# Adding the mask of the decay matrices on VectorE instead of multiplying it in on TensorE

## The reference

```python
a_cs = jnp.cumsum(dtc * a, axis=2)
seg = a_cs[:, :, :, None] - a_cs[:, :, None, :]
lower = jnp.tril(jnp.ones((L, L), dtype=bool))[None, None, :, :, None, None]
decay = jnp.exp(jnp.where(lower, seg, -jnp.inf))
cb = jnp.einsum('bclgn,bcsgn->bclsg', cc, bc)
y_diag = jnp.einsum('bclsg,bclsgr,bcsgrp->bclgrp', cb, decay, xd)
...
y = y_fwd + y_bwd + xs * d_skip
```

## Time and profile before

| | before |
|---|---|
| median of 3 runs | 1845.61 us (1844.77 to 1845.63) |
| the profiled execution's own time | 1845.08 us |
| span of the profiled execution | 1843.3 us |
| TensorE busy | 1828.3 us (99%) |
| TensorE weight loads busy | 1628.1 us (88%) |
| VectorE busy | 1266.7 us (69%) |
| ScalarE busy | 1055.9 us (57%) |
| granted TensorE clock | 1.00 over the whole span |

### The profile page before, as it was taken

How to read it: one execution, slowest core, us unless ns; L and a number is a source line. 1 busy time by engine, 2 the same in 40 slices (tenths; PEclk the granted TensorE clock), 3 DMA queues, 4 the chain that set the end, 5 groups by cost and what they waited for, 6 DMA issues and landing times.

```text
span 1843.3 us, 28625 instructions
## 1 busy us (share of the span) xinstructions
PE 1828.3 (99%) x11626; PEld 1628.1 (88%) x11626; DVE 1266.7 (69%) x1944; ACT 1055.9 (57%) x1557; POOL 100.5 (5%) x85
## 2 busy tenths in 40 slices
PE   9999999999999999999999999999999999999999
PEld 9998998789998999899789998988878888887887
DVE  6764797766665665588876665687667567875755
ACT  6444767565444444576755544475776456568642
POOL 0000110000000000020000000002001000210100
PEclk9999999999999999999999999999999999999999
DMA  8555542345555556553325555554445555534553
GB/s 292 193 191 182 188 151 100 106 137 189 192 193 186 190 195 194 180 179 112 126 92 172 191 193 189 173 184 147 139 137 182 194 163 182 171 126 137 172 192 116
DMA packets 86596, 310.09 MB, mean 168 GB/s; under 512 B 9648, under 2 KB 10288, under 8 KB 86464
## 3 DMA queue, kind: packets, MB, share of 16 engines
q1 hardware_dynamic: 85680, 306.35, 50.7%
q0 software_dynamic: 496, 1.65, 0.2%
q10 hardware_dynamic: 288, 0.25, 0.0%
HBM read 307.16 MB, written 1.05 MB: 167 GB/s over the span
## 4 chain that ended last, share of the span: by engine, by line
PE 95%; ACT 3%; DVE 1%; issue 0%; DMA 0%; POOL 0%; SPq 0%; DVEq 0%; ACTq 0%
PE bank L1162 92%; PE bank L1159 3%; ACT PA L1579 1%; DVE PA L2686 0%; ACT MP L1579 0%; ACT WH L1579 0%; ACT L1579 0%; DVE WL L2034 0%; DMA X<-in_x_dram 0%; ACT ET L1579 0%; DVE PC L2711 0%; DVE STATS L2384 0%; ACT BZ L1579 0%; DVE BO L2676 0%; DVE X L2120 0%
## 5 line engine op out<-in xcount | busy, mean ns | idle before, releaser
L2034 DVE TENSOR_TENSOR WL<-RAW,WH 128x1024 fp32r<-128x1024 f32 x585 | 704.6, 1213 | 405.0 <-ACT WH L1579 403.4
L1579 ACT ACTIVATE WH<-RAW 128x1024 fp32r<-128x1024 f32 (+2 forms) x587 | 610.1, 1050 | 497.0 <-PE bank L1162 494.2
L1162 PE MATMUL bank<-WH,FR 128*128 128x512 f32 x1264 | 318.4, 390 | 0.0
L1162 PEld LDWEIGHTS bank<-WH,FR 128*128 128x128 f32 x1264 | 233.7, 188 | 48.4 <-issue 0.8
L1162 PE MATMUL bank<-XTH,WH 128*128 128x256 f32 x1792 | 254.4, 279 | 0.6 <-ACT XTH L1579 0.6
L1162 PE MATMUL bank<-XTH,WL 128*128 128x256 f32 x1792 | 251.9, 278 | 0.0
L1162 PE MATMUL bank<-XTL,WH 128*128 128x256 f32 x1792 | 251.1, 277 | 0.0
L1162 PEld LDWEIGHTS bank<-XTH,WH 128*128 128x128 f32 x1792 | 226.9, 188 | 1.5 <-issue 0.8
L1162 PEld LDWEIGHTS bank<-XTH,WL 128*128 128x128 f32 x1792 | 226.7, 188 | 0.0
L1162 PEld LDWEIGHTS bank<-XTL,WH 128*128 128x128 f32 x1792 | 226.0, 188 | 0.0
L1162 PE MATMUL bank<-WL,FR 128*128 128x512 f32 x632 | 173.7, 389 | 0.0
(11 more groups left out here) (337 smaller groups left out, 1850.6 us busy)
## 6 DMA issues: line engine op xcount, KB each, us to landing
RAW<-in_WALL_dram SPq DMA_DIRECT2D x569, 512.0 KB, 3.3
RAW<-in_WALL_dram SPq DMA_DIRECT2D x8, 448.0 KB, 3.3
RAW<-in_WALL_dram SPq DMA_DIRECT2D x8, 256.0 KB, 2.6
X<-in_x_dram SPq DMA_DIRECT2D x4, 256.0 KB, 5.5
out_dram<-X SPq DMA_DIRECT2D x4, 256.0 KB, 2.0
ROWP<-in_ROWP_dram POOLq DMA_DIRECT2D x1, 672.0 KB, 11.0
CONSTS<-in_CST_dram POOLq DMA_DIRECT2D x1, 664.0 KB, 7.9
ROUNDED<-in_CSTR_dram POOLq DMA_DIRECT2D x1, 208.0 KB, 12.2
```

Source lines behind the costliest of these rows:

```text
L1162: return self.e.matmul(out, lhs, rhs, start=start, stop=stop, skip_group_check=True)
L1579: return self.e.activation(out, in_, func, **k)
L2034: self.e.tensor_tensor(lo, raw, hi.bitcast(F32), ALU.subtract).then_inc(*self.up("lo", j))
```

## The change

The mask product on TensorE goes. The bank is laid out by head, then direction, so that the two `TO` products write contiguous halves and the first of them opens the accumulation; the other two now write strided. VectorE reads the finished bank, adds the mask (broadcast over the two heads) and writes ET in SBUF: this is the VectorE part of `seg`, and it, in place of ScalarE's exponential, frees the bank and waits for the slot of ET. ScalarE exponentiates ET in place. That and the two operations of VectorE that follow make a new phase `exps`, which the planner places by itself. The costs that the planner sees change with it, from P53 A61 V90 in one phase to P40 V71 and A61 V90.

```diff
-"seg": "P53 A61 V90"
+"seg": "P40 V71", "exps": "A61 V90"
-    "seg": "exp"
+    "exps": "exp"
-FREES = {"seg": "A", "as": "V"}
+FREES = {"as": "V"}
...
         def segment(n):
             yield [("seg", i, n)]
+            yield [("exps", i, n)]
             if n:
                 yield "apply", i, n - 1
...
     # TensorE
-        b, bank = self.tbank(("seg", i, n), "et_act", (i, n))
-        ps = bank[:, :].rearrange("p (d x s) -> p d x s", d=2, x=2)
+        b, bank = self.tbank(("seg", i, n), "cut_dve", (i, n))
+        ps = bank[:, :].rearrange("p (x d s) -> p x d s", d=2, x=2)
-        self.mm(ps, k.EYER, k.CUT.unsqueeze(2).to_broadcast([128, 2, 2, 128]), True, False)
...
-            self.mm(ps[:, :, x, :], k.TO[:, h0 + x:h0 + x + 1].to_broadcast([128, 128]),
-                    k.LBH[:, 256 * t:256 * t + 256].rearrange("p (d s) -> p d s", d=2), False, False)
+            self.mm(ps[:, x, :, :], k.TO[:, h0 + x:h0 + x + 1].to_broadcast([128, 128]),
+                    k.LBH[:, 256 * t:256 * t + 256].rearrange("p (d s) -> p d s", d=2), x == 0, False)
...
     # apply reads the sum of the directions at columns 256 * x instead of 128 * x
...
     # ScalarE
-    def seg(self, i, n):
-        w.wait_ge(*self.at("seg_pe", (i, n)))
-        if n >= 4:
-            w.wait_ge(*self.at("apply_pe", (i, n - 4)))
-        else:
-            w.wait_ge(*self.at("fin_pe", (i, 1, 1)))
-        self.act(k.ET[:, n % 4, :], k.PS[k.bank["seg", i, n]][:, :], ACT.Exp).then_inc(*self.up("et_act", (i, n)))
+    def exps(self, i, n):
+        w.wait_ge(*self.at("cut_dve", (i, n)))
+        self.act(k.ET[:, n % 4, :], k.ET[:, n % 4, :], ACT.Exp).then_inc(*self.up("et_act", (i, n)))
...
     # VectorE
+    def seg(self, i, n):
+        cut = k.CUT.rearrange("p d s -> p (d s)").bitcast(F32).unsqueeze(1).to_broadcast([128, 2, 256])
+        w.wait_ge(*self.at("const5", 0))
+        w.wait_ge(*self.at("seg_pe", (i, n)))
+        if n >= 4:
+            w.wait_ge(*self.at("apply_pe", (i, n - 4)))
+        else:
+            w.wait_ge(*self.at("fin_pe", (i, 1, 1)))
+        e.tensor_tensor(k.ET[:, n % 4, :].rearrange("p (x e) -> p x e", x=2),
+                        k.PS[k.bank["seg", i, n]][:, :].rearrange("p (x e) -> p x e", x=2), cut, ALU.add).then_inc(
+            *self.up("cut_dve", (i, n)))
```

More of the change, by code:

```diff
@@ L190 @@
 TABLE = {
-    "decay0": "exp", "decay3": "log", "ex": "exp", "sc": "exp", "seg": "exp", "cn_a": "sqrt", "conv_silu": "silu",
+    "decay0": "exp", "decay3": "log", "ex": "exp", "sc": "exp", "exps": "exp", "cn_a": "sqrt", "conv_silu": "silu",
     "silu": "silu", "evict_z": "silu", "rope": "sin", "chain0": "exp", "chain7": "exp", "lam0": "exp", "mse": "exp",
@@ L1442, in apply @@
             h = 8 * g + 2 * q + x
-            m = self.mm(k.PS[t][:, 64 * (h % 8):64 * (h % 8) + 64], k.ET[:, n % 4, 128 * x:128 * x + 128],
+            m = self.mm(k.PS[t][:, 64 * (h % 8):64 * (h % 8) + 64], k.ET[:, n % 4, 256 * x:256 * x + 128],
                         k.XS[:, t, 64 * h:64 * h + 64], h % 8 == 0, True)
@@ L1568, in program @@
             "cn_split": self.cn_split, "qk_sq": self.qk_sq, "qkt": self.qkt, "sc": self.sc, "pt": self.pt, "mo_sq": self.mo_sq, "cum": self.cum,
-            "ex": self.ex, "xs": self.xs, "btk": self.btk, "cbm": self.cbm, "state": self.state, "seg": self.seg,
+            "ex": self.ex, "xs": self.xs, "btk": self.btk, "cbm": self.cbm, "state": self.state, "exps": self.exps,
             "fin_y": self.fin_y, "fin_norm": self.fin_norm, "chain": self.chain, "lam": self.lam, "hconv": self.hconv,
@@ L1996, in program @@
             "mo_a": self.mo_a, "mo_var": self.mo_var, "mo_y": self.mo_y, "cum": self.cum,
-            "state_x": self.state_x, "fin": self.fin, "seg": self.seg, "skip": self.skip, "mid": self.mid, "fin_y": self.fin_y,
+            "state_x": self.state_x, "fin": self.fin, "seg": self.seg, "exps": self.exps, "skip": self.skip, "mid": self.mid, "fin_y": self.fin_y,
             "fin_var": self.fin_var, "ift": self.ift, "chain": self.chain, "lam": self.lam, "rope2": self.rope2,
@@ L2444, in fin, with exps @@
             *self.up("fin_dve", (i, t, g, 0)))
+    def exps(self, i, n):
+        k, w, e = self.k, self.w, self.e
+        g, t = n // 8, n // 4 % 2
+        two = k.ET[:, n % 4, :].rearrange("p (x e) -> p x e", x=2)
+        own = two[:, :, 0:128]
+        w.wait_ge(*self.at("et_act", (i, n)))
+        e.tensor_tensor(own, own, two[:, :, 128:256], ALU.add).then_inc(*self.up("et_dve"))
+        w.wait_ge(*self.now("et_dve"))
+        w.wait_ge(*self.at("cbm_act", i))
+        e.tensor_tensor(own, own, k.CB[:, t, g, :].unsqueeze(1).to_broadcast([128, 2, 128]), ALU.mult).then_inc(
+            *self.up("et_dve", (i, n)))
     def seg(self, i, n):
         k, w, e = self.k, self.w, self.e
[L2448 to L2456, removed]
+        cut = k.CUT.rearrange("p d s -> p (d s)").bitcast(F32).unsqueeze(1).to_broadcast([128, 2, 256])
[8 more added lines that the diff above has]
+            *self.up("cut_dve", (i, n)))
     def skip(self, i, t):
```

2 lines of the change are left out of this document (1 added, 1 removed), and 2 rows, old and new, of the table WORK.

## The result

The changed kernel takes 1859.67 us (median of 4 runs, 1859.30 to 1861.64) against 1845.44 us for the kernel before (4 runs): the ratio is 1.008, interval 1.0068 to 1.0093, so 14.2 us slower. The forecast was 1842.1 us, its range ended at 1847.5, and 0.10 stood on slower.

The account below looks back on a forecast made before the run. TensorE, busy 99%, was taken as the bound: 7.0 us of masks saved, half lost waiting for VectorE, so 3.5 us off the median 1845.6 gives 1842.1 us. The 8-in-10 range was 1838.0 to 1847.5.

Parts of the forecast that it names:

- VectorE's balance: Each mixer's segment window: 40.0 us of VectorE work at 95.5 to 98.9% busy, a gain of 1.0 to 2.5 us.
- The length of the way: Segment's way from TensorE to its apply: 1.45 us before, 2.14 after, covered by a 2.5 us block; nothing taken.
- outer bound, 15 us: Segments' longer way, if uncovered: 0.47 us for each of 32, 15 us in all; chance 0.03.
- Splits leaving: Each mixer's segment window: three of VectorE's seven splits leave, taking out 3.7 us, made up behind it.
- third rival: Mixers: VectorE becomes the bound and costs more than the masks, splits staying in the window; 1846.6 to 1851.4 us, chance 0.16.
- The masks: TensorE in both mixers: 32 mask products removed at 0.22 us each, 7.0 us saved in all.
- The clock: Both mixers' segment windows: granted clock 1.00, playing no part in the sum.
- Outside the window: Behind each segment window: splits made up where VectorE has 5.3 us free; no added TensorE idle time counted.
- The durations: Segments: VectorE additions of 0.69 us, ScalarE exponential 0 to 0.04 us longer than 595 ns, sum of directions unchanged.
- fourth table load: ScalarE in each mixer: a possible further table load of 1.28 us beyond three, put at 0; a sign of being wrong.

Follow-up runs that it names:

- j1: Kernel before without its mask product, old order, plus an unawaited VectorE product of 512 constant columns behind each segment's product with cb; 1858.92 us, ratio 1.0068.
- e1: Kernel before without its mask product, nothing in its place, every engine in the old order; 1842.12 us, ratio 0.9978.
- h4: Kernel before without its mask product, old order, plus a VectorE product with ones and zeros between exponential and sum; 1863.36 us, ratio 1.0097.
- j2: Kernel before without its mask product, old order, plus a GpSimd fill of 640 columns between exponential and sum; 1849.71 us, ratio 1.0022.
- h3: Changed kernel with the splits of either mixer's segments moved back by two in the order; 1859.41 us, ratio 1.0075.
- e2: Changed kernel, same order, with the mask product put back on TensorE as well, so the mask is added twice; 1860.79 us, ratio 1.008.
- f1: Changed kernel, TensorE and VectorE order kept, exponential straight from the bank, an equal VectorE addition left that nobody waits for; 1868.28 us, ratio 1.0126.
- f2: Changed kernel, TensorE and VectorE order kept, exponential straight from the bank, addition dropped, no mask anywhere; 1863.63 us, ratio 1.0098.

## Why the prediction was wrong

**The step that failed: VectorE's balance.** "VectorE is busy 32.69 us of it and has 10.2 us free" took for free what has a price. 7.4 of those 10.2 us stand in the earlier trace rows as idle time ahead of the sums, ended by ScalarE's exponentials. The prediction showed this row and used its durations alone. Such time can be filled only by making the sums, and with them the apply, late: the changed kernel filled it (0.1 us left), and TensorE idled 4.4 us in each stretch and 3.2 and 2.8 behind it, where 1 to 2.5 us a mixer were forecast. In j1, against e1, VectorE did 7.8 us more in the first stretch (40.7 for 32.9), and the stretch grew by 5.9 us. The prediction then asked how full VectorE can get and took 95.5 to 98.9% from the stretch ahead of the segments. In the stretch itself it reached 89% in the changed kernel, with 47.2 us of work in place of 40.0, 85% in j1 and 83% in h4. With 40.0 us of work, 89 to 85% make a stretch of 44.9 to 47.1 us, 2 to 4 us a mixer longer than before in place of 1.0 to 2.5 shorter. These shares hold the lowered clock too: without the estimated 1.6, 5.3 and 5.0 us that it cost, they would be 91, 96 and 92%. How full VectorE could get at a clock of 1.00 throughout is therefore open.

**The length of the way.** "The length alone is covered" and "I take nothing for the length" were the second failure: j2 puts it at 5.8 us for 1.2 us more of way, 0.63 us of it the fill itself. The way was also mis-sized: 1.45 us before and 2.14 after add up the durations alone, while the runs have 1.9 and 4.4, with the waits in the queues. The prediction's outer bound, 15 us, was never part of a rival but for a chance of 0.03.

**Splits leaving.** Three were to leave the stretch; ten were made in it in place of seven, while three blocks of products moved in. The sign that the prediction named for the third rival, seven splits and a window over 42.9 us, came, and was exceeded. But h3, with one split fewer in each stretch, gained nothing.

**The masks.** 7.0 us were forecast, 3.5 came out (e1), and in the changed kernel 1.1 to 3.5 (e2). The Trainium skill's figure, by which the prediction had put the masks at an estimated 4.2 us ("TensorE: Matmul & The Clock Gate", "Back-to-back issue gap"), lies within the interval of 2.4 to 5.9, and mine doesn't. That doesn't bear the figure out, since the rows show 0.21 us and more a product and none shows 131 ns. What the runs do show is that the clock was lowered in both stretches of e1; the second, TensorE alone, beside the first above:

```profile
921.67:963.54 41.87, 40.88 (x238) 0.96 0.27 88
```

0.04 x (41.90 + 41.87) = 3.4 us went back there (an estimate), and idle time rose from 15.0 to 1840.7 - 1824.4 = 16.3 us. With the clock's share added back the masks come to 6.9 us. So the price of a product was about right, and what the sum lacked was the clock.

**The clock.** "The granted clock is 1.00 in both and plays no part" held for the kernel before alone. By the mean granted clock of the span, 0.996, the changed kernel loses some 0.004 x 1858 = 7 us to it (an estimate, since the clock is given to three digits). That is as much as the masks were to give, and its busy time didn't fall with them. So three terms make up the 14 us: the masks' 7 us less, the clock's 7 us more, and 14.2 us more of idle time.

**Outside the window.** The 3.2 and 2.8 us of idle time behind the stretches weren't in the sum: three blocks that stood there before had moved into the stretches.

**What was right.** The durations (684 ns forecast as 690, the exponential 632 as up to 631, the sum unchanged), no fourth table load in the stretch, nothing outside the mixers, and that VectorE's queue decides. The third rival had that mechanism, with the price of over-full work alone, 1846.6 to 1851.4 us; without the way, the crossings and the clock it ended 8 us short.

**What stays open.** The shares in the changed kernel's own order. Why the clock falls in one run and not in another is open, too. In the old order load and way are 14.9 and 5.8 us of the 20.5; in the new one f1 and f2, which were meant to part them, were spoiled by an order made for other work. How far a still better order could go wasn't settled by eight; that none beat 1857.9 us, and that a step of 0.63 us on the idle GpSimd alone already took 1849.7 us (j2), speaks against this change in any form tried here. No version that does the whole work beat the kernel before.

## What to carry to other kernels

Before work is moved to an engine with free time, look in its groups at what ends that idle time: waits in an in-order queue for a partner that works in turns with it are no free room, since work put there makes the partner's chain late. A step put into a chain with few items under way costs twice, by its load on the engine and by its length, and here the two added up to within some 3 us; measure them apart by putting the load behind the chain, and the length on an engine that has nothing to do. Read the granted clock beside every such comparison: waiting and a lowered clock are two costs. And when an order is written out beforehand, an experiment that removes work must let it be written anew or start from the order that was fitted to what is left.

## What the hardware did that I had not expected

**How much idle time a stretch holds doesn't tell what the clock does.** f2_no_add idled 7.0 us in the first stretch at a clock of 1.00 throughout and 7.0 us in the second at 0.97; e1_no_mask idled 1.0 us at 0.96. In e1 TensorE was busy 1.73 us of 364 to 366 and throughout from 366 to 368, and in the latter the clock fell; in the first stretch of f2 it was busy 3.06 and 3.23 of 5, and the clock stayed. First e1, then f2, with its second stretch last:

```profile
364.00:366.00 2.00, 1.73 (x9) 1.00 0.29 119
```

```profile
370.00:375.00 5.00, 3.06 (x18) 1.00 0.22 85
380.00:385.00 5.00, 3.23 (x22) 1.00 0.30 105
```

```profile
932.79:988.81 56.02, 48.97 (x274) 40.31 (x274) 37.71 (x69) 30.01 (x47) 1.64 (x3) 0.97 0.27 91
```

What parts these cases no run here settles.

**The first microseconds of an execution vary.** The same split, the 49th, far ahead of any mixer and the same in both kernels, starts at 129.17 us in the profiled execution of the kernel before and at 131.85 in that of j2; most of the difference, 2.4 of 2.7 us, is there at the ninth split (24 us), and behind the 49th it stays as it is up to the mixer:

```profile
129.17 1.23 DVE L2034 TENSOR_TENSOR WL<-RAW,WH 128x1024 fp32r<-128x1024 f32 x1 [1.50 <-ACT WH L1579]
```

```profile
131.85 1.23 DVE L2033 TENSOR_TENSOR WL<-RAW,WH 128x1024 fp32r<-128x1024 f32 x1 [1.49 <-ACT WH L1578]
```

Over the nineteen profiled executions it lies between -0.1 and +2.9 us against the kernel before. Whoever compares single executions by their span compares this too.
